# A decoder layer on one core: the stores of the MLP's operand forms are asked for by ScalarE's DMA queue instead of GpSimd's

## The chip, the cores and the metric

The kernel runs on one core of a Trainium2 chip. The metric is the device time of one execution in microseconds, taken as the median of several runs. The engines of the core are TensorE (PE), VectorE (DVE), ScalarE (ACT), GpSimd (POOL) and SyncE (SP). ACT, POOL and SP can each ask for DMA transfers, and all transfers run on the core's 16 DMA engines.

## The reference

One hybrid decoder layer in float32, for one sequence of 512 tokens, model width 2048, feed-forward width 8192. All inputs and the output are float32.

```
mod = silu(c) @ w_ada + b_ada                    # shift, scale, gate for the mixer and the MLP
h   = rms_norm(x, g_pre_mix) * (1 + sc1) + sh1
...                                              # RG-LRU group and forgetting attention over h @ w_in
x   = x + gt1 * rms_norm(y, g_post_mix)
h   = rms_norm(x, g_pre_mlp) * (1 + sc2) + sh2
y   = square(relu(h @ w_ff1)) @ w_ff2            # w_ff1 (2048, 8192), w_ff2 (8192, 2048)
x   = x + gt2 * rms_norm(y, g_post_mlp)
```

The change touches only the MLP, which takes some two thirds of the time and is done last.

## The kernel before

**Precision.** Every float32 factor of a product is split into a high part (a copy rounded to TensorE's fp32r) and a low part (the rest), and a product is three matmuls: low by high, high by low, high by high. ACT makes the high part of a weight tile, DVE subtracts to make the low part (`w_hi`, `w_lo`, a ring of RING = 4 slots). Such a tile is a *unit*; `high(n)` on ACT and `low(n)` on DVE prepare unit n, PE counts `unit_used` up when it is done with one.

**The MLP's stages.** Both MLP products are done with a Strassen-like scheme of seven products (P1, P5, P6, P3, P7, P2, P4) on 2 by 2 blocks, so that sums and differences of blocks are multiplied too.

- Units U_MLP to U_A - 1 (16 units) do the first 1024 columns of w_ff1 in plain form; they fill 4 *blocks* of 256 feed-forward rows (blocks 0 to 3). Meanwhile the operands `T12` and `T34` of the seven products are made from the activations, by `t_sums` (DVE), `t_high` (ACT) and `t_low` (DVE).
- Stage A, units U_A to U_B - 1 (28 blocks of 7 units) does the other 28 blocks of w_ff1.
- Stage B, units U_B to U_END - 1 (16 groups of 14 units), does w_ff2.

**What happens to a block b of the first product.** ACT reads it out of PSUM with a relu (`rectify_conv` or `rectify`) into `u_forms` (block 1: into `rows_base`), squares it, DVE forms the sums (`operand_sums`), so that there are seven forms of 128 x 256; ACT makes the high part of all seven in one instruction into a staging tile (`operand_high`: `hi_stage`; for blocks 0 and 1 two pieces of `T12` that are still free), DVE makes the low part in place (`operand_low`). Then both parts, 896 KB each, are stored to the DRAM tensor `u_scratch`, from which SP loads them back as stage B's stationary operands (`op`). In that tensor one form of one block is a run of 256 floats, 1 KB, per partition. There is one `u_forms` and one `hi_stage`: the next block's `rectify` waits on ACT until both stores of the block before it have landed (`stored_through(act, b - 1)`), and `t_high(2)` and `t_high(3)` wait for the stores of blocks 1 and 0. On each engine instructions run in program order, so whatever stands behind such a wait is held too.

**Order.** It is written out by hand as one loop over units per engine. ACT's loop in stage A and B:

```
for n in range(U_A, U_END):
    if U_A < n <= U_B and a_unit(n - 1)[1] in (P1, P5, P6):
        copy_sum(n - 1)
    if n + 3 < U_END:
        high(n + 3)
    for b, at in CLOSE_AT.items():
        if n - U_A == at:
            (rectify_conv if b < FIRST else rectify)(b)
            square_u(b)
        elif n - U_A == at + 2:
            operand_high(b)
```

`CLOSE_AT` gives the unit at which a block is closed: 0, 5, 10, 15 for blocks 2 to 5, then every 7 units, and 196 (which is U_B) for the last block, 31. POOL's program ends with the 64 stores in order of blocks (high, then low), each behind a wait for the part, then the loads of G2 and of the residual rows for the tail. SP's program holds the weight loads: in stage A one tile of 1 MB in 1 KB runs about every 10 us, at the start of stage B seven operand loads of 1 MB in 8 KB runs and the w_ff2 tiles of 1 MB in 2 KB runs.

Of the kernel before, what the change touches and what calls it, by code (L numbers as in the profile page):

```python
# [16 lines left out]
F32 = mybir.dt.float32  # L17
# [15 lines left out]
def hybrid_layer(nc, x, c, w_ada, b_ada, g_pre_mix, g_post_mix, g_pre_mlp, g_post_mlp, w_in, conv_w, conv_b,  # L33
# [78 lines left out]
    BLOCKS = D_FF // 256  # L112
    FIRST = 4
    U_A = U_MLP + CONV
# [17 lines left out]
    def a_unit(n):  # L132

        return divmod(n - U_A, 7)

    def b_unit(n):

        g, s = divmod(n - U_B, 14)
        return g, KINDS[g][s // 2], s % 2

    def sum_count(n):

        if n < U_B:
            blk, pos = a_unit(n)
            return 4 * blk + pos
        g, kind, h = b_unit(n)
        return 4 * (BLOCKS - FIRST) + 8 * g + 2 * SUM_INDEX[kind] + h + 1

    def made_of_sums(n):

        if n >= U_END:
            return False
        if n < U_B:
            return 1 <= a_unit(n)[1] <= 4
        return b_unit(n)[1] in SUM_INDEX
# [44 lines left out]
    with ExitStack() as ctx:  # L200
# [3 lines left out]
        def sem(name):  # L204
            return ctx.enter_context(nc.semaphore(name))

        def overlay(*specs):

            with ExitStack() as phase:
                return [phase.enter_context(nc.sbuf_tensor(n, s, d)) for n, s, d in specs]  # L210
# [48 lines left out]
        _, T34, u_forms, ext, T12, hsO = overlay(  # L259
            ("pad5", [P, 32 * 256], F32), ("T34", [P, 8, 2, 2, 256], F32R), ("u_forms", [P, 8, 256], F32), ("ext", [P, 4 * COLS], F32),  # L260
            ("T12", [P, 8, 2, 2, 256], F32R), ("hsO", [P, 2, 8, 2, 256], F32R))
# [40 lines left out]
        def forms_of(b):  # L302

            return rows_base[:, :, :].rearrange("p a (s n) -> p (a s) n", n=256) if b == 1 else u_forms[:, :, :]

        def stage_of(b):

            if b >= 2:
                return hi_stage[:, :, :]
            pair = (6, 4)[b]  # L310
            return T12[:, pair:pair + 2].rearrange("p j t a n -> p (j t a) n")[:, 0:7, :]

        def a_source(n):

            blk, pos = a_unit(n)
            even, odd = k_tile[2 * blk % 3], k_tile[(2 * blk + 1) % 3]
            return (even[:, :, 0:P], a_sum[0], a_sum[1], a_sum[0], a_sum[1], odd[:, :, 0:P], odd[:, :, P:2 * P])[pos]

        def by_tile(w, n):

            return w[:, n % RING, :].rearrange("p (j n) -> p j n", n=P)

        def b_source(n):

            g, kind, h = b_unit(n)
            return {P1: b_tile[0], P3: b_tile[2], P2: b_tile[3], P7: b_tile[1]}.get(kind, b_sum)[:, h, :]

        def tile_count(kappa):

            return 16 * (kappa // 3 + 1)  # L330

        def b_loaded(engine, which, g):

            if which < 2:
                engine.wait_ge(w2_in[which], 16 * (g + 1))
            else:
                engine.wait_ge(tile_in[which - 2], 16 * (19 + g + 1))

        def stored_through(engine, b):

            engine.wait_ge(u_stored[b % 2], 32 * (b // 2 + 1))
# [8 lines left out]
        def a_bank(blk, pos):  # L350

            return banks[4 * (blk % 2) + {P3: 1, P5: 1, P2: 2}.get(pos, 0)][:, 0:256]
# [5 lines left out]
        with ExitStack() as whole:  # L358
# [8 lines left out]
        u_scr = nc.dram_tensor("u_scratch", [8, P, 7, 2, 4, 256], F32, kind="Internal").ap()  # L367
# [53 lines left out]
        u_stored = [sem(f"u_stored{i}") for i in range(2)]  # L421
# [3 lines left out]
        relu_done, u_done, u_sum, op_hi_ready, op_lo_ready = (  # L425
            sem(n) for n in ("relu_done", "u_done", "u_sum", "op_hi_ready", "op_lo_ready"))
# [757 lines left out]
        def _(act):  # L1184
# [8 lines left out]
            def hi_part(n):  # L1193
                slot, count, s = unit(n)
                act.wait_ge(raw_in[slot], count)
                if n >= RING:
                    act.wait_ge(unit_used, n - RING + 1)
                cells = slice(0, 2 * width(n))
                act.activation(w_hi[:, s, cells], raw[:, slot, cells], ACT.Copy).then_inc(hi_ready, 1)  # L1199
# [342 lines left out]
            def square_u(b):  # L1542

                act.wait_ge(relu_done, b + 1)
                u = forms_of(b)[:, 0:4, :]
                act.activation(u, u, ACT.Square).then_inc(u_done, 1)

            def operand_high(b):

                act.wait_ge(u_sum, 4 * b + 4)  # L1550
                if b >= 2:
                    if b > 2:
                        stored_through(act, b - 1)
                    act.wait_ge(unit_used, U_A)
                act.activation(stage_of(b), forms_of(b)[:, 1:8, :], ACT.Copy).then_inc(op_hi_ready, 1)

            def copy_sum(n):

                blk, pos = a_unit(n)
                act.wait_ge(unit_used, n + 1)  # L1560
                act.activation(c_sums[:, blk % 2, {P1: 1, P5: 2, P6: 0}[pos], :], a_bank(blk, pos), ACT.Copy).then_inc(c_copied, 1)

            def high(n):

                if n < U_A:
                    return hi_part(n)
                if n < U_B:
                    blk, pos = a_unit(n)
                    if pos == P1:
                        act.wait_ge(tile_in[2 * blk % 3], tile_count(2 * blk))  # L1570
                    elif made_of_sums(n):
                        act.wait_ge(w_sum, sum_count(n))
                    else:
                        act.wait_ge(tile_in[(2 * blk + 1) % 3], tile_count(2 * blk + 1))
                    dst, w = by_tile(w_hi, n), a_source(n)
                else:
                    g, kind, h = b_unit(n)
                    if made_of_sums(n):
                        act.wait_ge(w_sum, sum_count(n))
                    else:  # L1580
                        b_loaded(act, {P1: 0, P3: 2, P2: 3}[kind], g)
                    dst, w = w_hi[:, n % RING, :], b_source(n)
                act.wait_ge(unit_used, n - RING + 1)
                act.activation(dst, w, ACT.Copy).then_inc(hi_ready, 1)  # L1584
# [27 lines left out]
            operand_high(0)  # L1612
            operand_high(1)
            high(U_MLP + 12)
            high(U_MLP + 13)
            high(U_MLP + 14)
            t_high(2)
# [7 lines left out]
            def final_square(t, src, width, i):  # L1625

                if squares[0]:
                    act.wait_ge(f_ssq, squares[0])
                dst = junk3[:, :, :] if width == 2 else junk3[:, 0, :]
                act.activation(dst, src, ACT.Square, accum_out=stat[:, FS + 4 * t + i:FS + 4 * t + i + 1]).then_inc(f_ssq, 1)  # L1630
                squares[0] += 1
# [9 lines left out]
# [8 lines that stand above are left out]
                        square_u(b)  # L1649
                    elif n - U_A == at + 2:  # L1650
                        operand_high(b)
                tail = n - G_LAST
                if 1 <= tail <= 4:
                    if tail == 1:
                        act.wait_ge(y_read, 7 * (GROUPS - 1))
                    final_square(tail - 1, tile_cols(y2[:, tail - 1, :], 0), 2, 0)
                if tail == 9:
                    act.wait_ge(y_read, 7 * (GROUPS - 1) + 4)
                    square_piece(0, 1)
                    square_piece(1, 1)  # L1660
                if tail == 11:
                    act.wait_ge(y_read, 7 * (GROUPS - 1) + 5)
                    square_piece(0, 0)
                    square_piece(1, 0)
# [686 lines left out]
        def _(pool):  # L2351
# [125 lines left out]
                pool.dma_start(x1_scr[t * P:(t + 1) * P, :], yg[:, t, :]).then_inc(x1_stored, 16)  # L2477
            store_gate(7)

            def store_forms(b):  # L2480

                K, i = divmod(b, 4)
                pool.wait_ge(op_hi_ready, b + 1)
                pool.dma_start(u_scr[K, :, :, 0, i, :], stage_of(b).bitcast(F32)).then_inc(u_stored[b % 2], 16)
                pool.wait_ge(op_lo_ready, b + 1)
                pool.dma_start(u_scr[K, :, :, 1, i, :], forms_of(b)[:, 1:8, :]).then_inc(u_stored[b % 2], 16)

            for b in range(BLOCKS):
                store_forms(b)
            pool.wait_ge(gate_stored, 16 * 8)  # L2490
            pool.wait_ge(unit_used, U_B)
            pool.dma_start(G2[:, :], gate_scr[1:2, :].to_broadcast([P, D])).then_inc(g2_in, 16)
# [32 lines left out]
```

## Time and profile before

| | us |
|---|---|
| median of 3 runs | 2055.84 (2055.41 to 2057.77) |
| the profiled execution, its own time | 2057.89 |
| its span in the trace | 2056.1 |
| PE busy | 1999.9 (97%) |
| DVE busy | 1738.8 (85%) |
| ACT busy | 950.6 (46%) |
| POOL busy | 142.0 (7%) |
| POOL: the 64 operand stores' issues | about 60 |
| SP's DMA queue: share of 16 engines' span | 52.6% |
| POOL's DMA queue | 10.2% |
| ACT's DMA queue | 0.7% |

The span is what the profiler sees from the first to the last instruction. The queue called q1 in the profile is SP's, q10 is ACT's, q0 is POOL's. A wait is written in square brackets behind the instruction that waited, with the work that ended it.

### The profile page before, as it was taken

Reading aid. Unit: us, or ns where it says so; the run is one execution under the profiler, and the core shown is the slowest. Engines: PE = TensorE matmul, PEld = TensorE weight load, DVE = VectorE, ACT = ScalarE, POOL = GpSimd, SP = SyncE. Lnnn points to the kernel's source line nnn. Section 1 sums busy time; section 2 is a strip of 40 time slices with the busy share of each in tenths; the row PEclk is TensorE's granted clock in tenths of the full one; section 3 lists DMA queues with packets and bytes.
Section 4 is the critical chain, followed back from the end, with each engine's and each line's share of the span. In section 5 each row is a group of like instructions: output and inputs, shape, how many; then the busy total and the mean of one; then the engine's idle time right before and its main releaser. Section 6 shows DMA issues by size and latency. Waiting matters only on the chain.

```text
span 2056.1 us, 28074 instructions
## 1 busy us (share of the span) xinstructions
PE 1999.9 (97%) x11091; PEld 1730.9 (84%) x11091; DVE 1738.8 (85%) x2010; ACT 950.6 (46%) x1208; POOL 142.0 (7%) x160
## 2 busy tenths in 40 slices
PE   7999999999999999889999999999999999999997
PEld 5787788888778778789999999998788888888885
DVE  7999897786988787778888888887888888888889
ACT  6434632124543366455656565655333333333334
POOL 2001120000220000011010010100000000000000
PEclk9999999999999999999999999999999999999998
DMA  9986668966348744365665656567866556556542
GB/s 368 392 280 192 203 196 292 298 181 205 122 166 274 269 167 161 123 200 191 203 207 178 211 183 203 196 198 281 313 221 246 173 195 245 188 182 244 203 165 102
DMA packets 231843, 442.99 MB, mean 215 GB/s; under 512 B 12600, under 2 KB 106984, under 8 KB 222240
## 3 DMA queue, kind: packets, MB, share of 16 engines
q1 hardware_dynamic: 208416, 360.79, 52.6%
q0 software_dynamic: 18928, 75.68, 10.2%
q10 hardware_dynamic: 4368, 4.73, 0.7%
q8 instruction: 88, 1.44, 0.3%
q14 instruction: 43, 0.35, 0.0%
HBM read 371.92 MB, written 69.24 MB: 215 GB/s over the span
## 4 chain that ended last, share of the span: by engine, by line
PE 51%; DVE 4%; DMA 3%; issue 1%; ACT 1%; DVEq 0%; SPq 0%; ACTq 0%
PE pair L1143 9%; PE pair L1145 9%; PE pair L1144 9%; PE bank L1125 8%; PE bank L1127 8%; PE bank L1126 8%; DMA u_scratch<-u_forms 1%; DVE w_lo L2139 1%; DMA w_tiles<-in_w_ff_dram 1%; DMA raw<-in_w_ff_dram 1%; DVE u_forms L2128 0%; DVE y L2213 0%; DVE rows_base L2186 0%; DVE raw L2186 0%; DVE y L2267 0%
## 5 line engine op out<-in xcount | busy, mean ns | idle before, releaser
L1143 PE MATMUL pair<-w_hi,op 128*128 128x512 f32 x896 | 350.0, 391 | 4.3 <-DVE w_lo L2139 2.3
L1144 PE MATMUL pair<-w_lo,op 128*128 128x512 f32 x896 | 349.3, 390 | 0.0
L1145 PE MATMUL pair<-w_hi,op 128*128 128x512 f32 x896 | 349.2, 390 | 0.0
L1584 ACT ACTIVATE w_hi<-raw 128x1024 fp32r<-128x1024 f32 x183 | 193.6, 1059 | 234.9 <-PE pair L1145 184.0
L1199 ACT ACTIVATE w_hi<-raw 128x1024 fp32r<-128x1024 f32 (+1 forms) x130 | 135.0, 1045 | 281.4 <-DMA raw<-in_w_in_dram 166.3
L1125 PE MATMUL bank<-T,w_lo 128*128 128x256 f32 x896 | 254.7, 284 | 6.4 <-DVE c_sums L2194 6.0
L1126 PE MATMUL bank<-T,w_hi 128*128 128x256 f32 x896 | 254.4, 284 | 0.0
L1127 PE MATMUL bank<-T,w_hi 128*128 128x256 f32 x896 | 254.3, 284 | 0.0
L2139 DVE TENSOR_TENSOR w_lo<-raw,w_hi 128x1024 fp32r<-128x1024 f32 x183 | 223.0, 1220 | 27.7 <-ACT w_hi L1584 27.7
L1724 DVE SCALAR_TENSOR_TENSOR rows_base<-raw,cc,rows_base 128x512 f32<-128x512 f32 x224 | 178.2, 796 | 29.7 <-DMA raw<-in_w_ada_dram 19.6
L1143 PEld LDWEIGHTS pair<-w_hi,op 128*128 128x128 f32 x896 | 168.6, 188 | 40.9 <-DVE w_lo L2139 3.1
L675 PE MATMUL bank<-h_hi,w_lo 128*128 128x512 f32 x496 | 198.0, 399 | 0.3
L1145 PEld LDWEIGHTS pair<-w_hi,op 128*128 128x128 f32 x896 | 168.7, 188 | 35.1
L1144 PEld LDWEIGHTS pair<-w_lo,op 128*128 128x128 f32 x896 | 168.6, 188 | 35.1 <-issue 0.2
L1692 DVE TENSOR_TENSOR w_lo<-raw,w_hi 128x1024 fp32r<-128x1024 f32 (+1 forms) x129 | 162.1, 1258 | 42.6 <-ACT w_hi L1199 41.1
L677 PE MATMUL bank<-h_hi,w_hi 128*128 128x512 f32 x496 | 193.7, 391 | 0.0
L676 PE MATMUL bank<-h_lo,w_hi 128*128 128x512 f32 x496 | 193.7, 391 | 0.0
L1584 ACT ACTIVATE w_hi<-rows_base 128x1024 fp32r<-128x1024 f32 x112 | 118.8, 1062 | 157.0 <-PE bank L1127 137.0
L1125 PEld LDWEIGHTS bank<-T,w_lo 128*128 128x128 f32 x896 | 172.9, 193 | 6.8 <-DVE w_lo L2139 6.2
L1126 PEld LDWEIGHTS bank<-T,w_hi 128*128 128x128 f32 x896 | 173.0, 193 | 0.0
L1127 PEld LDWEIGHTS bank<-T,w_hi 128*128 128x128 f32 x896 | 172.9, 193 | 0.0
L2213 DVE TENSOR_TENSOR y<-y,pair 128x1024 f32<-128x1024 f32 x104 | 126.5, 1217 | 14.2 <-PE pair L1145 14.2
(346 smaller groups left out, 4204.3 us busy)
## 6 DMA issues: line engine op xcount, KB each, us to landing
raw<-in_w_ada_dram SPq DMA_DIRECT2D x128, 512.0 KB, 4.7
op<-u_scratch SPq DMA_DIRECT2D x56, 1024.0 KB, 7.2
raw<-in_w_ff_dram SPq DMA_DIRECT2D x53, 1024.0 KB, 6.2
raw<-in_w_in_dram SPq DMA_DIRECT2D x74, 512.0 KB, 4.7
ext<-in_w_ff_dram SPq DMA_DIRECT2D x35, 1024.0 KB, 6.8
gst<-in_w_ada_dram SPq DMA_DIRECT2D x64, 512.0 KB, 8.3
w_tiles<-in_w_ff_dram SPq DMA_DIRECT2D x32, 1024.0 KB, 7.0
u_scratch<-u_forms POOLq DMA_DIRECT2D x31, 896.0 KB, 6.8
```

What stands on the lines that cost most here:

```text
L675: pe.matmul(b[:, :], lo[:, cols], act_hi[:, kt, :], start=(kt == first), stop=False)
L676: pe.matmul(b[:, :], hi[:, cols], act_lo[:, kt, :], start=False, stop=False)
L677: last = pe.matmul(b[:, :], hi[:, cols], act_hi[:, kt, :], start=False, stop=(kt == n_kt - 1))
L1125: pe.matmul(out_, lo, moving(pos, j, 0), start=(fresh and j == 0), stop=False, skip_group_check=True)
L1126: pe.matmul(out_, hi, moving(pos, j, 1), start=False, stop=False, skip_group_check=True)
L1127: last = pe.matmul(out_, hi, moving(pos, j, 0), start=False, stop=(j == 7), skip_group_check=True)
L1143: pe.matmul(bank[:, tt, :], op_lo, hi, start=(start and fresh and h == 0 and k == 0), stop=False, skip_group_check=True)
L1144: pe.matmul(bank[:, tt, :], op_hi, lo, start=False, stop=False, skip_group_check=True)
L1145: last = pe.matmul(bank[:, tt, :], op_hi, hi, start=False, stop=(h == 1 and k == 1), skip_group_check=True)
L1584: act.activation(dst, w, ACT.Copy).then_inc(hi_ready, 1)
L1724: ins = dve.scalar_tensor_tensor(a, row, cc[:, 2, k:k + 1], a if k else acc_init[:, :], ALU.mult, ALU.add)
L2139: dve.tensor_tensor(out_, w, hi.bitcast(F32), ALU.subtract).then_inc(lo_ready, 1)
```

## The change

The function that stores a block's forms moves from POOL's program to ACT's and is cut in two: `store_forms(b, 0)` stores the high part, `store_forms(b, 1)` the low part. For blocks 0 and 1 all four stores stand behind `high(U_MLP + 12)`, first both high parts, then both low parts. For every later block the high part's store stands one unit behind `operand_high` (at + 3) and the low part's two units behind (at + 4), each at the end of its unit, behind that unit's `high(n + 3)`. One thing differs in what is stored: the low part's source is `u_forms` for every block, where it was `rows_base` for block 1; number and size of the transfers are as before. The waits of others on `u_stored` are unchanged.

```diff
+            def store_forms(b, part):
+
+                K, i = divmod(b, 4)
+                act.wait_ge((op_hi_ready, op_lo_ready)[part], b + 1)
+                src = u_forms[:, 1:8, :] if part else stage_of(b).bitcast(F32)
+                act.dma_start(u_scr[K, :, :, part, i, :], src).then_inc(u_stored[b % 2], 16)
...
             high(U_MLP + 12)
+            for part in range(2):
+                store_forms(0, part)
+                store_forms(1, part)
...
                     elif n - U_A == at + 2:
                         operand_high(b)
+                    elif n - U_A in (at + 3, at + 4):
+                        store_forms(b, n - U_A - at - 3)
...
-            def store_forms(b):
-
-                K, i = divmod(b, 4)
-                pool.wait_ge(op_hi_ready, b + 1)
-                pool.dma_start(u_scr[K, :, :, 0, i, :], stage_of(b).bitcast(F32)).then_inc(u_stored[b % 2], 16)
-                pool.wait_ge(op_lo_ready, b + 1)
-                pool.dma_start(u_scr[K, :, :, 1, i, :], forms_of(b)[:, 1:8, :]).then_inc(u_stored[b % 2], 16)
-
-            for b in range(BLOCKS):
-                store_forms(b)
```

On ACT, at the end of the 16 plain units, the piece of the order before (L1555 is `operand_high` of blocks 0 and 1, L1199 is `high`, L1512 and L1513 are `t_high(2)`):

```order
L1555 ACTIVATE T<-u_forms 128x1792
L1555 ACTIVATE T<-rows_base 128x1792
L1199 ACTIVATE w_hi<-raw 128x1024 x3
L1512 ACTIVATE T<-ext 128x2x2x256
L1513 ACTIVATE T<-ext 128x2x2x256
```

and the same place now (L1562 is `store_forms`):

```order
L1555 ACTIVATE T<-u_forms 128x1792
L1555 ACTIVATE T<-rows_base 128x1792
L1199 ACTIVATE w_hi<-raw 128x1024
L1562 DMA u_scratch<-T 896x1x256 x2
L1562 DMA u_scratch<-u_forms 896x1x256 x2
L1199 ACTIVATE w_hi<-raw 128x1024 x2
L1512 ACTIVATE T<-ext 128x2x2x256
L1513 ACTIVATE T<-ext 128x2x2x256
```

Four stores, 896 runs of 256 floats each, now stand between the first and the second of the three `high`, and ahead of `t_high(2)`, which waits for two of them.

On ACT, at the border of stages A and B, before (L1555 is `operand_high(30)`, L1561 `copy_sum`, L1584 `high`, L1538, L1540 and L1546 are `rectify(31)` and its square):

```order
L1555 ACTIVATE hi_stage<-u_forms 128x1792
L1561 ACTIVATE c_sums<-bank 128x256
L1584 ACTIVATE w_hi<-ext 128x1024
L1584 ACTIVATE w_hi<-w_tiles 128x1024 x2
L1584 ACTIVATE w_hi<-raw 128x1024 x2
L1538 ACTIVATE u_forms<-bank 128x256
L1540 ACTIVATE u_forms<-c_sums 128x768
L1546 ACTIVATE u_forms<-u_forms 128x1024
L1584 ACTIVATE w_hi<-raw 128x1024 x2
```

and now (`copy_sum` is L1568 and `high` is L1591 here):

```order
L1555 ACTIVATE hi_stage<-u_forms 128x1792
L1568 ACTIVATE c_sums<-bank 128x256
L1591 ACTIVATE w_hi<-ext 128x1024
L1562 DMA u_scratch<-hi_stage 896x1x256
L1591 ACTIVATE w_hi<-w_tiles 128x1024
L1562 DMA u_scratch<-u_forms 896x1x256
L1591 ACTIVATE w_hi<-w_tiles 128x1024
L1591 ACTIVATE w_hi<-raw 128x1024 x2
L1538 ACTIVATE u_forms<-bank 128x256
L1540 ACTIVATE u_forms<-c_sums 128x768
L1546 ACTIVATE u_forms<-u_forms 128x1024
L1591 ACTIVATE w_hi<-raw 128x1024 x2
```

The two stores of block 30 stand behind one and two `high`; the relu of block 31, which waits for both to land, keeps its place, and two `high` stand right behind it.

## Rows read from the trace of the kernel before

**Rows 1.** Busy time of each engine by stretch, with counts, PEclk, DMA share, GB/s

```profile
890.00:900.00 10.00, 7.13 (x44) 7.16 (x45) 9.86 (x13) 5.27 (x5) 1.87 (x2) 0.66 0.22 92
...
960.00:1000.00 40.00, 40.00 (x336) 40.00 (x335) 34.60 (x38) 23.85 (x28) 3.75 (x4) 1.00 0.62 199
```

**Rows 2.** Timeline of PE: start, duration, instruction, and the idle time before it

```profile
841.77 0.79 PE L1047 MATMUL pair<-hsE,w_lo 128*128 128x512 f32 x1 [5.53 <-DVE w_lo L1692]
...
892.87 0.55 PE L1125 MATMUL bank<-T,w_lo 128*128 128x256 f32 x1 [6.03 <-DVE c_sums L2194]
...
1437.34 0.50 PE L1143 MATMUL pair<-w_hi,op 128*128 128x512 f32 x1 [2.05 <-DVE y L2211]
...
1469.62 0.50 PE L1143 MATMUL pair<-w_hi,op 128*128 128x512 f32 x1 [1.94 <-DVE w_lo L2139]
```

**Rows 3.** Timeline of ACT: the instructions that waited for a store to land

```profile
822.19 1.06 ACT L1512 ACTIVATE T<-ext 128x1024 fp32r<-128x1024 f32 x1 [8.04 <-DMA u_scratch<-rows_base]
...
867.54 1.23 ACT L1527 ACTIVATE u_forms<-pair 128x512 f32<-128x512 f32 x2 [2.57 <-DMA u_scratch<-u_forms]
...
887.32 0.38 ACT L1538 ACTIVATE u_forms<-bank 128x256 f32<-128x256 f32 x1 [7.74 <-DMA u_scratch<-u_forms]
...
1428.79 0.38 ACT L1538 ACTIVATE u_forms<-bank 128x256 f32<-128x256 f32 x1 [3.91 <-DMA u_scratch<-u_forms]
```

**Rows 4.** Timelines of POOL and ACT at the stores of block 0

```profile
806.19 0.98 POOL L2484 DMA_DIRECT2D u_scratch<-T  x1 [27.56 <-ACT T L1555]
807.38 1.99 ACT L1199 ACTIVATE w_hi<-raw 128x1024 fp32r<-128x1024 f32 x2
```

**Rows 5.** Timelines of POOL, ACT and SP over one steady block of stage A

```profile
1011.44 0.93 POOL L2486 DMA_DIRECT2D u_scratch<-u_forms  x1 [1.12 <-DVE u_forms L2128]
1011.98 1.06 ACT L1584 ACTIVATE w_hi<-ext 128x1024 fp32r<-128x1024 f32 x1 [1.61 <-PE bank L1127]
1012.30 0.37 SPq L514 DMA_DIRECT2D raw<-in_w_ff_dram  x1
...
1021.59 0.37 ACT L1538 ACTIVATE u_forms<-bank 128x256 f32<-128x256 f32 x1
```

**Rows 6.** The page's DMA issues: count, KB each, median us from issue to landing

```profile
u_scratch<-u_forms POOLq DMA_DIRECT2D x31, 896.0 KB, 6.8
u_scratch<-hi_stage POOLq DMA_DIRECT2D x30, 896.0 KB, 4.4
...
k_scratch<-xnT ACTq DMA_DIRECT2D x2, 1024.0 KB, 8.4
```

**Rows 7.** DMA queues from 59 to 61 us: packets, MB, share of 16 engines

```profile
q10 hardware_dynamic: 264, 0.54, 69.3%
q1 hardware_dynamic: 265, 0.26, 36.5%
```

**Rows 8.** DMA queues from 1418 to 1421 us, the same columns

```profile
q1 hardware_dynamic: 91, 0.73, 70.7%
q0 software_dynamic: 84, 0.34, 27.8%
```

**Rows 9.** DMA issues from 1412 to 1430 us: count, KB each, us to landing

```profile
op<-u_scratch SPq DMA_DIRECT2D x7, 1024.0 KB, 14.2
raw<-in_w_ff_dram SPq DMA_DIRECT2D x1, 1024.0 KB, 16.7
ext<-in_w_ff_dram SPq DMA_DIRECT2D x1, 1024.0 KB, 16.1
...
u_scratch<-u_forms POOLq DMA_DIRECT2D x1, 896.0 KB, 14.1
```

**Rows 10.** Timelines of DVE and ACT at the start of stage B

```profile
1429.85 1.22 DVE L2186 TENSOR_TENSOR raw<-raw 128x1024 f32<-128x1024 f32 x1 [6.28 <-DMA raw<-in_w_ff_dram]
...
1433.46 0.42 DVE L2117 TENSOR_TENSOR u_forms<-u_forms 128x256 f32<-128x256 f32 x1
...
1430.09 1.06 ACT L1546 ACTIVATE u_forms<-u_forms 128x1024 f32<-128x1024 f32 x1
```

## The prediction, made before the changed kernel was run

> **What bounds the kernel now.** I read the table by stages first. In the middle of stage A, PE is busy without a gap, 40.00 of 40 us at full clock, and DVE at 34.6 and ACT at 23.9 have room [rows 1]. So anything that the change costs or saves can only show where PE idles: the reader should next see PE's timeline [rows 2]. Around the MLP it has four large gaps: 5.53 us at 841.8, 6.03 us at 892.9, and 2.05 and 1.94 us at 1437.3 and 1469.6. Then ACT's timeline [rows 3]: three of the gaps have a wait of ACT for a *store to land* some way ahead of them: 8.04 us at 822.2 (`t_high(2)`, for block 1's stores; DVE's work for the following units queues behind it), 7.74 us at 887.3 (`rectify(4)`), 3.91 us at 1428.8 (`rectify(31)`). From the second pair follows how much lateness ACT can absorb: it waited 7.74 us and PE 6.03 us, so about 1.7 us are free. The wait of 2.57 us at 867.5 cost PE nothing that the timeline shows.
>
> So the stores are not idle traffic. When they land decides five places, and the change moves both when they are asked for and in which queue they run.
>
> **Part 1: the issue itself.** 64 issues of 0.93 to 0.98 us leave POOL, which is idle otherwise; they are worth nothing there. On ACT a DMA issue shows up as a short entry in its queue, not as busy time, and behind each unit's `high` ACT waits 1.61 us for PE [rows 5]. An issue of up to a microsecond fits in that. I take 0 for all of them.
>
> **Part 2: the time of issue.** In a steady block the low part was asked for at 1011.44. Now it stands behind the `high` that starts at 1011.98 and takes 1.06, so at 1013.05: 1.6 us later. The high part moves some 1 us. The relu that waits for them is reached at 1021.59 [rows 5], 8.5 us behind the new issue. Asked for alone or nearly so, the stores landed after 4.4 us (high) and 6.8 us (low, with the high part's tail and a weight load beside it) [rows 6]. Landing takes longer now (part 3): high part, SP's tile of 1 MB and low part are together 2.9 MB from about 1012 on, at 0.36 to 0.40 MB per us [rows 7, 8] 7.2 to 8.1 us, and some 1.5 us until the last byte is confirmed: about 1021. I take 0 for the 25 blocks at a pitch of 7 units. The bound above: ACT's 1.7 us of slack on top of the 8.5, so a landing up to 10.2 us still costs nothing.
>
> For blocks 2 to 5 the pitch is 5 units, and ACT waits there already. Each store asked for 1 to 1.6 us later, with a slower landing, adds to 2.57 and 7.74 us; against this, the low parts of blocks 3 to 5 come out of DVE late anyhow and are asked for at the same time as before. I take +1 us in all, from -2 to +4.
>
> For blocks 0 and 1 the first store was asked for at 806.19; now it stands behind the first `high` of the two that start at 807.38, so at 808.4, 2.2 us later [rows 4]. The last of the four needs DVE's low part of block 1 and hardly moves. The four are 3.67 MB, and `t_high(2)` waits until the last two have landed, at 822.2. If the DMA engines are what limits, the delay of the first is the delay of the last: 2.2 us at most, less what ran slowly at first, plus what SP's next tile (asked for before they end) takes from them. I take +2, from 0 to +5. The whole chain behind `t_high(2)` hangs on it, so PE's gap at 841.8 grows by as much.
>
> **Part 3: the share of the DMA engines.** Here is the step on which most of my number rests. From 59 to 61 us a store of ACT's queue runs beside loads of SP's: 264 packets against 265, 0.54 MB against 0.26 [rows 7]. The engines take turns packet by packet, and a queue's share of bytes is its packet's share of size: 2 KB against 1 KB. A hardware queue's packet is one run, 1 KB for those loads. At the border of stages A and B [rows 8] POOL's queue moves 84 packets of 0.34 MB, 4 KB each, although the same tensor is stored in runs of 1 KB, beside 91 packets of 8 KB. So GpSimd's queue packs four runs in a turn. From ACT's queue I expect one run of 1 KB in a turn, as for SP's 1 KB loads.
>
> Count the turns for block 30's two stores: 2 x 896 runs on 16 engines are 112 turns each. SP has in its queue at that time, in this order, two operand loads, a w_ff2 tile, two operand loads, a tile, three operand loads [rows 9]. An operand load of 8 KB packets is 8 turns per engine, a tile of 2 KB packets 32. Sum: 16 + 32 + 16 + 32 + 24 = 120 turns, less a few already done when the stores begin. So 112 turns last until about the end of the seventh operand load. The bytes until then: 7 + 2 loads of 1.05 MB and 1.84 MB of stores, 11.3 MB, which at 0.40 MB per us take 28 us from about 1414.5: the low part lands at about **1443**. Before it took 14.1 us from 1414.64 [rows 9], to 1428.7.
>
> What is queued behind: `rectify(31)` on ACT starts 14.3 us later. DVE's four sums of block 31 and, behind them on DVE, the low part of PE's next unit and the first addition into y, wait for it. ACT's square ended at 1431.15 and the sums began at 1433.46 [rows 10], so 2.3 us are free: 12.0 us more of idle PE at the gap of 1437.3. After a gap of 6.03 us PE's granted clock was 0.66 over 10 us [rows 1], so about 6.8 us at 1.2 in place of 2.4 GHz, which loses 3.4 us; I charge that once. What comes back: the tile that DVE waited 6.28 us for [rows 10] arrives earlier, but DVE's in-order program is then held by the relu; and SP's backlog is worked off in the pause, so that the gap of 1.94 us later may close. I take -1.9. Together 12.0 + 3.4 - 1.9 = **+13.5**.
>
> The other end of this term: if a turn of ACT's queue carries as much as POOL's did, the store lands 1 to 2 us later than before for its later issue, inside the 2.3 us: 0. Above, at 0.36 MB per us, 11.3 MB take 31 us: +16.5. My value is near the upper end because the nearest rows (packets of hardware queues) are plain.
>
> The Trainium skill, page "DMA: Bandwidth & Descriptors", gives for the first byte about 1 us on GpSimd's path and 0.6 us on that of SyncE and ScalarE ("Specifications") and calls the latter generally faster. It speaks against my forecast. The nearest rows do not bear it out for these sizes: ACT's own stores of 1 MB landed after 8.4 us beside SP's loads, POOL's of 896 KB after 4.4 and 6.8 [rows 6].
>
> **Sum.** 0 (issues) + 0 (steady blocks) + 1 (blocks 2 to 5) + 2 (blocks 0 and 1) + 13.5 (block 30) = +16.5 us. On the profiled execution's own time, 2057.89 (span 2056.1, and 1.8 around it), that is 2074.4; the median of the runs shown is 2.05 lower, and the forecast is made for it: 2055.84 + 16.5 = **2072.3**. What a measurement of this kernel tells from no change is about 0.2%, 4 us.
>
> **Rivals.**
>
> *Stores land as before* (0.14). If ACT's queue also packs runs, or the engines' turns weigh bytes, only the issue times move: +1 to +3 for blocks 0 to 5, nothing at block 30. 2057 to 2059. For it speaks that all queues run on the same engines; against it rows 7 and 8. The same page of the Trainium skill says it of asking from several engines ("Issuing engines are not separate DMA queues"): it saves issue time and nothing else. By that the time would stay; rows 8 show that the share of a queue depends on how its packets are cut, which that sentence leaves open.
>
> *Faster: the stores land sooner* (0.06). Place: `t_high(2)` and `rectify(4)`, whose 8.04 and 7.74 us of waiting both reach PE. If descriptors made in hardware bring each of these forward by 1.5 us, each gap of PE shrinks by that: -3; and at the border SP's first tile comes 4 us sooner for the smaller share of the stores while block 30 still lands by 1431, which may close the gap of 2.05. 2051 to 2053. It decides from the point at which a store beside a load lands sooner than POOL's 6.8 us. Rows 6 speak against it. The page's latencies alone would make 0.4 us per store on the path, so -1 to -2.
>
> *Every block late* (0.08). Place: the 25 steady blocks. If the low part lands later than 10.2 us behind its issue, because SP's tile goes ahead and ACT's transfer starts late, every further microsecond costs 25 us. At 11.5 us that is +33 beside the rest: about 2105.
>
> *The forecast* (0.72): border of the stages, 2061 to 2086.
>
> **Numbers.** Likeliest 2072.3. Its own range follows from the bounds: terms of 0 to +5, -2 to +4, and 6 to 17 at the border, 2061 to 2084. The range for all goes down to 2055, so that it takes in most of the case without change, and up to 2084; outside are the faster case, the every-block case and a small tail. Slower 0.80 (forecast and every block late), same 0.13, faster 0.07.
>
> **What would show it.** In the changed kernel's profile: ACT's queue with 57 MB more in packets of 1 KB, and POOL's with as much less (right or wrong for part 3 at once). At the border, turns of ACT's queue and SP's alike in number and ACT's bytes a small part; `rectify(31)` starting near 1443 with a wait of some 15 us; a gap of PE of about 14 us behind it in place of 2.05, then a stretch at a granted clock near 0.5. `t_high(2)` some 2 us later. In the steady blocks PE at 100% as before. It would be wrong if ACT's packets are larger, if block 30 lands before 1433, or if gaps of PE appear once per block.

## The result: 11.6 us slower, and the profile after

| | before | after |
|---|---|---|
| median of the runs, us | 2055.62 (2054.95 to 2057.77, 4 runs) | 2067.18 (2066.80 to 2067.89, 4 runs) |
| profiled execution, its own time | 2057.89 | 2066.95 |
| span of it | 2056.1 | 2065.1 |

The ratio of after to before is 1.0055, with a 95% interval from 1.0037 to 1.0072. The forecast was 2072.3 with a range from 2055 to 2084: the sign and the place are as forecast, and the size is 5 us too large. The profiled execution of before was 2.3 us above its median, so the two profiled executions differ by 9.1 us and not by 11.6.

First the timeline of PE after, from 780 to 1500 us, the largest gaps; it answers to [rows 2]:

```profile
840.60 0.79 PE L1047 MATMUL pair<-hsE,w_lo 128*128 128x512 f32 x1 [5.62 <-DVE w_lo L1704]
...
892.85 0.55 PE L1125 MATMUL bank<-T,w_lo 128*128 128x256 f32 x1 [7.17 <-DVE c_sums L2206]
...
924.12 0.36 PE L1125 MATMUL bank<-T,w_lo 128*128 128x256 f32 x1 [0.69 <-ACT c_sums L1568]
...
1448.72 0.80 PE L1143 MATMUL pair<-w_hi,op 128*128 128x512 f32 x1 [15.22 <-DVE y L2223]
```

One gap stands out, and up to 1500 us it is the only one over 0.3 us behind the border of the stages: 15.22 us, where before had 2.05 and, 32 us later, 1.94 [rows 2]. All gaps over 0.3 us in this stretch sum to 29.13 us (one more, of 0.43, is not shown); before they sum to 18.41, with four small ones that are not among the rows (1.20, 0.88, 0.42 and 0.36).

Next the timeline of ACT after: the waits for a store to land, to be held against [rows 3].

```profile
820.92 1.06 ACT L1512 ACTIVATE T<-ext 128x1024 fp32r<-128x1024 f32 x1 [7.27 <-DMA u_scratch<-u_forms]
...
887.30 0.38 ACT L1538 ACTIVATE u_forms<-bank 128x256 f32<-128x256 f32 x1 [8.65 <-DMA u_scratch<-u_forms]
...
1442.46 0.38 ACT L1538 ACTIVATE u_forms<-bank 128x256 f32<-128x256 f32 x1 [18.71 <-DMA u_scratch<-u_forms]
```

`rectify(31)` started at 1442.46, and its wait is 14.8 us longer than before. The forecast had 1443. (The trace after is 1.1 us ahead of the trace before when it gets here, so counted from the same work it is 1443.6.) DVE is held by it, as its timeline at the border shows:

```profile
1444.84 0.42 DVE L2129 TENSOR_TENSOR u_forms<-u_forms 128x256 f32<-128x256 f32 x1 [14.99 <-ACT u_forms L1546]
...
1446.31 1.22 DVE L2151 TENSOR_TENSOR w_lo<-raw,w_hi 128x1024 fp32r<-128x1024 f32 x1
1447.45 1.22 DVE L2223 COPY y<-pair 128x1024 f32<-128x1024 f32 x1
```

The four sums of block 31 stand ahead of the low part of PE's next unit and of the first copy out of `pair` into y. PE is named as waiting for the latter: it needed the banks that this copy empties.

The queues on the page of after, and in two stretches at the border (1418 to 1421, then 1422 to 1427; packets, MB, share of 16 engines):

```profile
q10 hardware_dynamic: 62736, 63.45, 9.2%
q0 software_dynamic: 3568, 16.95, 2.2%
```

```profile
q1 hardware_dynamic: 254, 0.86, 74.5%
q10 hardware_dynamic: 258, 0.26, 24.7%
...
q1 hardware_dynamic: 401, 1.68, 81.6%
q10 hardware_dynamic: 410, 0.41, 23.2%
```

ACT's queue (q10) takes as many turns as SP's (q1), 258 against 254 and 410 against 401, and moves 1 KB in each: 0.26 MB where SP's moves 0.86. Before, POOL's queue moved 0.34 MB in 84 turns beside SP's 0.73 MB in 91 [rows 8].

One more transfer runs beside the stores, and it is an effect of the change that its description does not name. In POOL's program the load of G2 stood behind the 64 stores. With these gone it waits only for PE to reach stage B. The first line is from the trace before, the second from the trace after, the third from the answer on the DMA issues of after:

```profile
1441.38 0.77 POOL L2492 DMA_DIRECT2D G<-gate_scratch  x1
```

```profile
1423.15 0.55 POOL L2494 DMA_DIRECT2D G<-gate_scratch  x1 [645.03 <-PE bank L1127]
```

```profile
G<-gate_scratch POOLq DMA_DIRECT2D x1, 1024.0 KB, 9.4
```

So 1.05 MB that no instruction reads before 2010 us now land at 1432.5, while block 30's stores are under way, and ahead of their landing. From 1428 to 1432 us three queues take turns: 137 packets of SP's, 129 of ACT's, 113 of POOL's.

Last, windows of after (columns as in [rows 1]):

```profile
930.00:1420.00 490.00, 490.00 (x4085) 490.00 (x4085) 423.04 (x463) 287.15 (x339) 0.00 (x0) 1.00 0.61 198
...
1430.00:1440.00 10.00, 3.50 (x16) 2.57 (x14) 0.00 (x0) 0.00 (x0) 0.00 (x0) 0.93 1.04 413
1440.00:1450.00 10.00, 1.28 (x3) 1.09 (x4) 5.13 (x8) 7.47 (x8) 0.00 (x0) 0.50 0.69 278
1450.00:1460.00 10.00, 10.00 (x40) 8.11 (x40) 10.00 (x9) 3.37 (x4) 1.58 (x3) 0.89 0.69 234
```

The steady blocks are full, 490.00 of 490 us: 25 blocks with two stores each asked for by ACT cost nothing. From 1434 to 1440 us PE, DVE, ACT and POOL all stand still while the DMA engines run full (1.04 and 413 GB/s in the window from 1430): they work off the loads that SP had already asked for.

### The profile page after: what moved, and what is told of

Same layout as the page of the kernel before. It is cut to its first block, busy times and chain, and to the rows that moved or that the text cites. A ratio compares the mean times of both kernels' runs of the same rounds, so it can differ in the third digit from the quotient of the medians.

```text
span 2065.1 us, 28074 instructions
## 1 busy us (share of the span) xinstructions
PE 1999.9 (97%) x11091; PEld 1731.9 (84%) x11091; DVE 1738.4 (84%) x2010; ACT 950.0 (46%) x1208; POOL 81.4 (4%) x96
## 4 chain that ended last, share of the span: by engine, by line
PE 54%; DVE 2%; DMA 2%; issue 1%; ACT 0%; DVEq 0%; ACTq 0%
PE pair L1143 9%; PE pair L1144 9%; PE pair L1145 9%; PE bank L1125 9%; PE bank L1126 9%; PE bank L1127 9%; DMA u_scratch<-u_forms 2%; DVE w_lo L2151 1%; DVE y L2225 0%; DVE y L2279 0%; DVE x1r_a L2335 0%; ACT u_forms L1546 0%; PE pair L1047 0%; DVE x1r_b L2335 0%; DVE rows_base L2198 0%
## 5 line engine op out<-in xcount | busy, mean ns | idle before, releaser
L1591 ACT ACTIVATE w_hi<-raw 128x1024 fp32r<-128x1024 f32 x183 | 193.7, 1059 | 228.4 <-PE pair L1145 196.1
L1199 ACT ACTIVATE w_hi<-raw 128x1024 fp32r<-128x1024 f32 (+1 forms) x130 | 134.9, 1045 | 283.1 <-DMA raw<-in_w_in_dram 168.6
L1591 ACT ACTIVATE w_hi<-rows_base 128x1024 fp32r<-128x1024 f32 x112 | 118.8, 1062 | 156.9 <-PE bank L1127 136.4
```

## The experiments

All ratios are to the kernel before, run beside on the same chip. e1 to e4 shared its runs (median 2057.18), e5 to e7 (2055.65), and e8 and e9 (2056.67).

**e1 and e2: only block 30?** e1 is the changed kernel with the stores of blocks 30 and 31 given back to POOL (and block 1's low part stored from `rows_base` as before); e2 is the kernel before with block 30's two stores alone given to ACT.

```diff
 e1:
+    BY_ACT_STORE = range(0, 30)
...
-                    elif n - U_A in (at + 3, at + 4):
+                    elif b in BY_ACT_STORE and n - U_A in (at + 3, at + 4):
                         store_forms(b, n - U_A - at - 3)
 e2:
+    BY_ACT_STORE = (30,)
...
+                    elif b in BY_ACT_STORE and n - U_A in (at + 3, at + 4):
+                        store_forms(b, n - U_A - at - 3)
```

> Blocks 0 to 29 are stored by ACT's queue as in the changed kernel, blocks 30 and 31 by POOL's as before (behind a semaphore of their own; block 1's low part again from rows_base). Theory (turns): nearly all of the +11.5 us is block 30's two stores taking turns of 1 KB against SP's 8 KB and 2 KB; without them the wait of rectify(31) falls from 18.7 to about 4 us, PE's gap of 15.2 us to about 2, and the time is 2055.6 + what the early blocks changed (-0.7 us at t_high(2), +1.1 at block 4, -0.9 at block 5, +0.3 at block 6): 2055 to 2056. Rival (the early blocks or the steady ones cost something, the border only part of it): above 2059.

> The reverse: only block 30's two stores are in ACT's queue, every other block's in POOL's as before. Theory (turns): the landing of block 30's low part stays near 28 us, PE's gap near 15 us, the time near 2055.6 + 11 = 2067. Rival (the loss needs all blocks in ACT's queue, for example ACT's sequencer being held by its DMA issues, or a backlog): under 2059.

Measured: e1 2056.66 us, ratio 0.9998 (0.9989 to 1.0006); e2 2065.3 us, ratio 1.0038 (1.0024 to 1.0051). PE and ACT of e2 at the border:

```profile
1448.61 0.79 PE L1146 MATMUL pair<-w_hi,op 128*128 128x512 f32 x1 [13.22 <-DVE y L2223]
```

```profile
1442.35 0.38 ACT L1541 ACTIVATE u_forms<-bank 128x256 f32<-128x256 f32 x1 [16.71 <-DMA u_scratch<-u_forms]
```

Two stores of 64 bring 8.1 us, some 70% of the loss, and a border like that of the changed kernel; with those of blocks 30 and 31 given back nothing is left of it. A part of the 3.5 us between e2 and the changed kernel can be read off: in e2 POOL still asks for G2 behind block 31's stores, at 1452.65. Block 30's low part landed after 26.3 us there and after 28.3 in the changed kernel, and PE's gap is 13.22 in place of 15.22. So about 2 us of the loss go with G2's load, which the change set free (at 406 GB/s, as measured in this stretch, its 1.05 MB take 2.6 us). No run moved that load by itself. The other 1.5 us are within the intervals. So the 60 others cost nothing in ACT's queue that can be measured, and that takes away what I had charged to blocks 0 to 5.

**e3 and e4: is it the size of a packet?** Both lay `u_scratch` out so that a store is one run of 7 KB per partition; e3 from ACT's queue (the changed kernel), e4 from POOL's (the kernel before). The loads still read it in the old arrangement, so the second product of these two multiplies forms in another arrangement than the reference's.

```diff
+        u_rows = u_scr.rearrange("k p f a b n -> k p (f a b n)").rearrange("k p (j m) -> k p j m", j=8)
...
-                act.dma_start(u_scr[K, :, :, part, i, :], src)
+                act.dma_start(u_rows[K, :, 4 * part + i, :], src.rearrange("p f n -> p (f n)"))
```

> The changed kernel, with each store written to DRAM as one run of 7 KB per partition in place of seven of 1 KB; same bytes, same queue, same places in the program. The loads are as before, so they read the forms in another arrangement and what stage B computes is not the reference's product. Theory (turns): ACT's queue moves packets much larger than 1 KB, its share beside SP's 8 KB packets is near a half, block 30's stores land within 10 to 14 us, rectify(31) waits under 4 us, the time is 2053 to 2057. Rival (the transfer is late because it is asked for in ACT's queue, whose descriptors wait behind SP's, whatever the size of a run): landing near 28 us and 2067 as in the changed kernel.

> The control: the kernel before, with the same runs of 7 KB per partition in POOL's queue (the loads again read another arrangement, so stage B's product is not the reference's). Theory (turns): POOL's queue already packs about 4 KB in a turn, so little changes: 2054 to 2056.5, PE's gaps at the border within 1 us of those before. Rival (the run in DRAM, not the queue, decides the landing in any queue): a gain of several us, as large as that from the changed kernel to the same layout there, 2045 to 2050.

Measured: e3 2044.19 us, ratio 0.9935 (0.9920 to 0.9950); e4 2047.65 us, ratio 0.9951 (0.9937 to 0.9964). The border's gap is 1.61 us in e3, so the theory held where it was made for. But both came out well below what the theory had said, e3 by 9 us and e4 by 6. In e4 the number is the rival's (2045 to 2050): the length of the run helps in POOL's queue too, by 9.5 us, though less than the 23 us from the changed kernel to e3. I had looked at the border and not at what runs of 7 KB do for the stores before 930 us. In the page's DMA issues the low part's landing fell in both queues:

```profile
u_scratch<-u_forms ACTq DMA_DIRECT2D x32, 896.0 KB, 4.7
```

```profile
u_scratch<-u_forms POOLq DMA_DIRECT2D x31, 896.0 KB, 5.3
```

That is 4.7 us in e3 where after had 7.0, and 5.3 in e4 where before had 6.8 [rows 6].

**e5 and e6: the whole computation with 7 KB stores.** The same layout, and now each operand load picks its form out of it, as eight runs of 1 KB per partition in place of one of 8 KB. e5 from the changed kernel, e6 from the kernel before.

```diff
-                sp.dma_start(op[:, f].rearrange("p a b n -> p (a b n)").bitcast(F32), u_scr[K, :, f].rearrange("p a b n -> p (a b n)")
+                sp.dma_start(op[:, f].rearrange("p a b n -> p (a b) n").bitcast(F32), u_rows[K].rearrange("p j (f n) -> p j f n", f=7)[:, :, f, :]
```

> The changed kernel with u_scratch laid out by part, block within the group, form: each store is one run of 7 KB per partition as in e3_act_7kb_runs, and now the operand loads pick their form out of that layout, eight runs of 1 KB per partition in place of one of 8 KB, so that the whole computation is the reference's. A 1 KB packet took 46 ns and one of 8 KB 309 ns in this case's runs, so the op tiles need about 19% more of the DMA engines' time; stage B has 41% of it free. Theory (what costs is which packets meet at the border, and SP's lead over PE hides dearer loads): the stores land as in e3 or sooner, since SP's op packets no longer are the long ones, PE's gap at the border stays under 4 us, 2043 to 2049. Rival (the op tiles become the late thing at the border, seven of them in 1 KB packets against 7 KB packets of the stores): PE waits for op at 1430 to 1470, some 5 to 15 us in all, 2050 to 2062.

> The kernel before with the same layout of u_scratch and the same loads in 1 KB runs: POOL stores as in e4_pool_7kb_runs, the whole computation is the reference's. Theory: as e4, 2046 to 2051, so 1 to 4 us above e5. Rival as for e5: waits of PE for op at the border, 2053 to 2065.

Measured: **e5 2045.48 us, ratio 0.9947 (0.9934 to 0.9959)**, so 10 us faster than the kernel before; e6 2048.30 us, ratio 0.9964 (0.9952 to 0.9977). The dearer loads stay hidden: the one gap that waits for them is 0.72 us. PE of e5, all that is left over 0.7 us:

```profile
835.84 0.79 PE L1048 MATMUL pair<-hsE,w_lo 128*128 128x512 f32 x1 [3.44 <-DVE w_lo L1705]
883.17 0.36 PE L1126 MATMUL bank<-T,w_lo 128*128 128x256 f32 x1 [1.36 <-DVE c_sums L2207]
1411.55 0.47 PE L1144 MATMUL pair<-w_hi,op 128*128 128x512 f32 x1 [0.72 <-DMA op<-u_scratch]
1421.53 0.50 PE L1144 MATMUL pair<-w_hi,op 128*128 128x512 f32 x1 [1.55 <-DVE w_lo L2152]
1426.60 0.50 PE L1144 MATMUL pair<-w_hi,op 128*128 128x512 f32 x1 [2.04 <-DVE y L2224]
```

What 7 KB runs do before 930 us shows in two answers on the queues from 808 to 812 us, when the stores of blocks 0 and 1 are under way: after, then e5.

```profile
DMA packets 914, 1.17 MB, mean 291 GB/s; under 512 B 32, under 2 KB 658, under 8 KB 914
...
q10 hardware_dynamic: 642, 0.64, 61.3%
q1 hardware_dynamic: 272, 0.52, 36.8%
```

```profile
DMA packets 367, 1.68 MB, mean 421 GB/s; under 512 B 32, under 2 KB 32, under 8 KB 367
...
q10 hardware_dynamic: 211, 1.40, 83.2%
q1 hardware_dynamic: 156, 0.29, 19.3%
```

In the same 4 us ACT's queue moves 1.40 MB in place of 0.64. The engines moved 421 GB/s in place of 291 at a busy share near 1 in both, so short packets carried less in the same time; the rest is ACT's share of the bytes, 83% in place of 55%. The counts of packets are not equal here, since SP's queue was not backed up all the time: from 809 to 810 us after has 5 packets of it beside 204 of ACT's. So these rows do not show what the taking of turns is worth at this place.

The 2.8 us between e5 and e6 lie for the most part before 930 us too: PE's gaps at 835 and 883 us are 3.44 and 1.36 in e5, and 4.53 and 2.46 in e6. Whether ACT's earlier asking or its queue makes them is not shown.

**e7: 1 KB packets from POOL's queue.** The kernel before, with block 30's low part cut into seven stores, one per form, so that none has more than one run per partition.

```diff
+                if b == 30:
+                    for f in range(7):
+                        pool.dma_start(u_scr[K, :, f, 1, i, :], forms_of(b)[:, 1 + f, :]).then_inc(u_stored[b % 2], 16)
+                    return
```

> The kernel before, but the low part of block 30 is asked for by POOL as seven stores, one for each form: the same bytes in the same queue, each packet 1 KB, since no store has more than one run per partition. The last of the seven is asked for some 6 to 8 us after the one store of before. Theory (queues take turns packet by packet, and POOL's queue was quick because its packets were 4 KB): the low part lands near 1440 or later, ACT's wait before rectify(31) is 13 to 20 us and PE's gap at the border 10 to 17 us, 2066 to 2074. Rival (POOL's queue is served better than ACT's whatever its packets): only the later asking counts, the low part lands at most 8 us later, 1429 to 1436, gap 2 to 8 us, 2056 to 2062.

Measured: 2055.96 us, ratio 1.0003 (0.9994 to 1.0012). It did not make the packets that I wanted. POOL asked for the seven in 3.74 us:

```profile
1412.08 0.94 POOL L2484 DMA_DIRECT2D u_scratch<-hi_stage  x1 [17.17 <-ACT hi_stage L1555]
1414.14 3.74 POOL L2488 DMA_DIRECT2D u_scratch<-u_forms  x7 [1.11 <-DVE u_forms L2128]
```

and its queue had 19024 packets on the page where before had 18928. Had 896 KB gone out in 1 KB packets in place of 224 of 4 KB, it would be 672 more and not 96 (six more transfers on 16 engines, so one small packet for each would be all of it). The queue seems to pack runs of several partitions too, so the run tells nothing of the rival. It tells that spreading the asking over 3.74 us costs nothing.

**e8: SP's packets made small instead.** The other side of the same ratio: ACT's stores as in the changed kernel, but the tile `op` holds the two parts of a block side by side, so that an operand load is two transfers in 1 KB packets (PE's products index the tile accordingly).

```diff
-("op", [P, 7, 2, 4, 256], F32R)
+("op", [P, 7, 4, 2, 256], F32R)
...
+                for part in range(2):
+                    sp.dma_start(op[:, f, :, part, :].bitcast(F32), u_scr[K, :, f, part]).then_inc(op_in[kind], 16)
```

> The changed kernel with its stores untouched (1 KB packets in ACT's queue); only SP's loads of the operands differ: the tile op holds the two parts of a block side by side in SBUF, so a load is two transfers, one for each part, whose packets are 1 KB in place of 8 KB. The computation is the reference's. Theory (the queues take turns packet by packet, so a queue's share of the bytes goes with the size of its packets): beside op loads ACT's stores now get half of the bytes in place of a ninth; the low part of block 30 lands at 1426 to 1434 in place of 1442, PE's gap at the border is 1 to 7 us in place of 15.2, and the gaps at 840 and 892, where no op load runs, stay: 2053 to 2061. Rival (stores of 1 KB runs, 8 KB apart in DRAM, are slow in ACT's queue by themselves, whatever SP loads beside them): landing at 1439 or later, gap over 11 us, 2063 to 2069.

Measured: 2056.91 us, ratio 1.0000 (0.9991 to 1.0009). Not one store was touched, and the 11 us are gone. ACT's wait, PE's gaps, and the queues from 1420 to 1423 us:

```profile
1424.93 0.38 ACT L1538 ACTIVATE u_forms<-bank 128x256 f32<-128x256 f32 x1 [1.58 <-DMA u_scratch<-u_forms]
```

```profile
1432.77 0.50 PE L1143 MATMUL pair<-w_hi,op 128*128 128x512 f32 x1 [2.38 <-DVE w_lo L2151]
1437.83 0.50 PE L1143 MATMUL pair<-w_hi,op 128*128 128x512 f32 x1 [2.05 <-DVE y L2223]
```

```profile
q10 hardware_dynamic: 557, 0.57, 54.0%
q1 hardware_dynamic: 559, 0.56, 52.8%
```

In these 3 us there are again as many turns for one queue as for the other, 557 and 559, and now as many bytes. From 1414 to 1421 us it is 1317 against 1275 in sum, but single microseconds in it are far from equal (327 of ACT's to 26 of SP's from 1415, 96 to 286 from 1418), and no run says why. The gaps at 839 (5.65) and 892 (7.08), where no operand load runs, are those of the changed kernel, as expected.

**e9: only the last group in 7 KB runs.** The changed kernel, with the layout of e5 for blocks 28 to 31 alone; SP's loads at the border keep their 8 KB packets.

```diff
+                if K == 7:
+                    act.dma_start(u_rows[K, :, 4 * part + i, :], src.rearrange("p f n -> p (f n)")).then_inc(u_stored[b % 2], 16)
+                    return
```

> The changed kernel, but the four blocks of the last group (28 to 31) alone are stored as one run of 7 KB per partition, and the loads of that group, 60 us and more before they are needed at the end of stage B, pick their forms out in 1 KB runs; groups 0 to 6 are as in the changed kernel, and so are SP's loads at the border. The computation is the reference's. Theory (the border's 13 us hang on the size of the packets of block 30's stores alone): PE's gap at the border is 1.5 to 4 us, the gaps at 840 (5.6) and 892 (7.2) and ACT's waits there stay as in the changed kernel, 2052 to 2057, so some 8 to 11 us of what e5_act_runs_whole gained lie before 930. Rival (the border gains only because all the stores before it, or SP's dearer op loads, change what is under way): gap over 8 us, 2060 to 2069.

Measured: 2054.87 us, ratio 0.9991 (0.9982 to 1.0001). PE at the border, and the queues from 1418 to 1421 us:

```profile
1435.39 0.50 PE L1148 MATMUL pair<-w_hi,op 128*128 128x512 f32 x1 [1.41 <-DVE y L2231]
```

```profile
q1 hardware_dynamic: 97, 0.66, 56.2%
q10 hardware_dynamic: 96, 0.57, 45.6%
```

97 turns against 96, and 0.57 MB beside 0.66. The border's loss is gone by the stores' packets alone, as in e8 by the loads' alone; what e5 gains beyond e9, 9 us by the two ratios, lies for the most part before 930 us. From 780 to 930 us PE was idle for 13.9 us in e9 (136.11 busy of 150) and for 5.0 in e5 (145.03).

## Why the prediction was right, and what was mis-sized

**Part 1, issues worth nothing: right.** The steady stretch is full. The exact times were not those I gave: I had put each issue behind the `high` that stands ahead of it in ACT's program, some 1 and 1.6 us later than before. In the steady block of [rows 5] the low part was asked for at 1010.87, as the `high` ahead of it began at 1010.85, and that `high` stands 1.1 us earlier than in the trace before; so the issue moved by 0.6 us. The profile after shows that ACT's queue does not wait for the work ahead of it. At blocks 0 and 1:

```profile
805.29 1.69 ACT L1555 ACTIVATE T<-rows_base 128x1792 fp32r<-128x1792 f32 x1
805.42 0.60 ACTq L1562 DMA_DIRECT2D u_scratch<-T  x1
806.88 1.04 ACT L1199 ACTIVATE w_hi<-raw 128x1024 fp32r<-128x1024 f32 x1
807.01 0.55 ACTq L1562 DMA_DIRECT2D u_scratch<-T  x1
808.22 3.17 ACTq L1562 DMA_DIRECT2D u_scratch<-u_forms  x2
811.49 2.16 ACT L1199 ACTIVATE w_hi<-raw 128x1024 fp32r<-128x1024 f32 x2 [3.57 <-issue]
```

Block 0's high part was asked for at 805.42, as soon as its data was there, while the copy of block 1 ran and before the `high` at 806.88 that stands ahead of it in the program. What an issue holds up is the compute instruction behind it: the next `high` had an idle time of 3.57 us marked as issue. PE lost nothing by it here.

**Part 2, blocks 0 and 1: the term of +2 was wrong, about -0.7 measured.** It rested on the store being asked for 2.2 us later; it was asked for sooner (805.42, where before had 806.19 [rows 4]; 0.5 of these 0.8 us are the whole kernel being ahead at that place). ACT's wait at `t_high(2)` is 7.27 us where it was 8.04, and PE's gaps there are 0.43 and 5.62 where they were 1.20 and 5.53. Blocks 2 to 5, the term of +1: the gap at 892 grew from 6.03 to 7.17, the small ones shrank from 1.30 to 0.69, +0.5 in all.

**Part 3, the border: right in mechanism and in the landing (1442.4 for 1443), the term of +13.5 somewhat too large.** Its idle part was 12.0 - 1.9 = 10.1; measured is 15.22 in place of 2.05, 1.94 and 0.36, so 10.9, and the gap of 1.94 us did close. That the landing fits so well is in part luck. The sum of 11.3 MB had 9.4 MB of SP's loads and nothing of POOL's; from 1414.1 to 1442.4 us the queues moved 8.57 MB of SP's, 1.05 of POOL's (G2) and 1.84 of ACT's, 11.5 in all. Two errors of about 1 MB cancel.

The clock part, 3.4, was mis-sized, and this is the step that failed most. I had read it from a granted clock of 0.66 over ten microseconds [rows 1], but PE was idle for 2.87 of these; it ran only about 4 us at the lower level, until 897, which costs 2.0. After the change the granted clock is 0.50 in the ten microseconds in which PE restarts, of which it ran 1.28, and 0.89 in the next ten: 0.6 + 1.1 = 1.7 us. And before paid as much at this border, behind its gap of 1.94 us:

```profile
1470.00:1480.00 10.00, 10.00 (x39) 8.11 (x38) 9.90 (x10) 4.36 (x5) 0.00 (x0) 0.83 0.64 210
```

A granted clock of 0.83 over ten busy microseconds loses 1.7 us. That gap is gone after the change, so the clock adds nothing, and PE's busy time is 1999.9 us on both pages.

**The sum.** In the profiled executions: -0.7 + 0.5 + 10.9 = 10.7 us of idle time. The spans differ by 9.0; the rest is that PE was busy for 758.87 of the first 780 us after and for 757.13 before, a stretch that the change does not touch. The medians differ by 11.6, since before's profiled execution was one of its slower ones. Of the 16.5 forecast, 2.7 were the wrong sign of the term of +2, 0.5 the term of +1, and 3.4 the clock; 0.8 more idle time at the border goes the other way. The forecast's own range, given as 2061 to 2084, was added to the profiled execution's time; from its bounds (4 to 26 us) and the median it is 2060 to 2082. And the bytes that moved to ACT's queue are 58.7 MB, not 57.

**The rivals.** "Stores land as before" falls by the landing, 28.3 us after the issue. "Faster" was right in one detail, a sooner `t_high(2)`, worth 0.7 us of PE's gaps and not the 1.5 that it named for that place; `rectify(4)` waited longer (8.65 for 7.74). "Every block late" falls by the full window. The page "DMA: Bandwidth & Descriptors" of the Trainium skill, section "Issuing engine by pattern", calls the path of SyncE and ScalarE generally faster; this case's trace does not agree for 1 KB runs beside 8 KB loads (11.6 us slower), and does for 7 KB runs (e5 is 2.8 us below e6, whatever the reason). Its section "Queues, rings and completion order" says that a DMA engine takes turns between queues a packet at a time; the counts at the border agree (254 to 258 and 401 to 410 after, 97 to 96 in e9, 557 to 559 in e8). It gives 9 to 17 descriptors as typical for one packet; no run here shows how the profile's packets stand to those.

**Shown and argued.** Shown: the loss is that of block 30's stores (e1, e2); it goes when either side of the ratio of packets is changed alone (e8, e9); in these stretches at the border, with both queues backed up, turns are nearly equal in number. That is not so in every stretch: it fails where one queue is not backed up (808 to 812 us), and in single microseconds of e8. Argued only: the 2 us that go with G2's load (e2 beside the changed kernel, no run of its own); that the issues run ahead because only data is waited for, seen in the timeline and not tried apart. Open: how POOL's queue would fare with packets of 1 KB, since e7 did not make any.

## What to carry to other kernels

When two queues are both backed up, count turns and not bytes: a store in short runs beside loads in long ones gets the share of its packet (1 KB beside packets of 2 and 8 KB: a fifth to a quarter of the bytes here), and whatever waits for it waits for the other queue's backlog. Before moving a transfer to another queue, read the size of its packets in either; if something waits for it, give it long runs in DRAM, and let the side that is fetched early pay with the short ones (e5: 10 us faster than the kernel before, though 56 loads of 1.05 MB go in 1 KB runs). And look for where the queues meet: 60 of the 64 stores moved at no cost that can be measured (e1), and the two of block 30 cost most of it (e2). Last, when transfers leave a program, look at what stood behind them: G2's load came 18 us earlier and into the way.

## What was not expected of the hardware

- POOL's queue sent 4 KB packets even for stores that had one 1 KB run per partition (96 packets more for seven stores in place of one, where 1 KB packets would be 672 more); ACT's queue sent every run by itself. The pages bear it out: the change takes 15360 packets from POOL's queue, 240 per store (224 of 4 KB and 16 more), and gives ACT's queue 58368, 912 per store (896 of 1 KB and 16 more).
- ACT's DMA issues ran 1.5 us ahead of the compute instruction that stands before them in its program (805.42 against 806.88), and two issues together could take 3.17 us where the first two took 0.60 and 0.55.
- SP's loads in 1 KB runs hold SP itself: in e8 four issues at the border took 6.68 us, where in the changed kernel two of 8 KB runs took 0.82. That spaces out SP's backlog, so a part of what e5 and e8 gain at the border may be this and not the share of turns; e9, whose loads there are as in the changed kernel, has the same gain without it.

The rows for the last point, SP's timeline in e8 and then in the changed kernel:

```profile
1419.35 6.68 SPq L530 DMA_DIRECT2D op<-u_scratch  x4
```

```profile
1419.74 0.82 SPq L529 DMA_DIRECT2D op<-u_scratch  x2
```
